# One kernel of three transformer blocks: the expert stage split further and loaded by halves, and a small store issued by another engine

## Time and profile before

| | |
|---|---|
| median of 3 runs | 3319.97 us (3319.68 to 3324.28) |
| profiled execution | 3321.52 us, span 3319.7 us |
| mean granted TensorE clock | 0.965 |
| TensorE busy | 3104.9 us, 94% |
| VectorE, ScalarE, GpSimd busy | 1830.9, 1596.4, 737.2 us |
| DMA | 693.72 MB, mean 209 GB/s |

### The profile page before, as it was taken

One profiled execution on the slowest core, in us unless ns is written; L12 is line 12 of the kernel. 1 busy time (PEld: TensorE's weight loads), 2 busy tenths in 40 slices (PEclk: granted clock), 3 DMA queues, 4 the chain that ended last, 5 costly groups with the idle time before them and its releaser, 6 DMA issues. The chain is left out here.

```text
span 3319.7 us, 39152 instructions
## 1 busy us (share of the span) xinstructions
PE 3104.9 (94%) x14036; PEld 2408.6 (73%) x14036; DVE 1830.9 (55%) x2216; ACT 1596.4 (48%) x2141; POOL 737.2 (22%) x379
## 2 busy tenths in 40 slices
PE   7986999998999999989997888999999999999997
PEld 6754678877877787768885666777777777777753
DVE  3257433344367404440031447887888888888773
ACT  4334434433566423232231325766766766666652
POOL 2400144442523344324442330000000000000020
PEclk9987999999999999999998898999999999999998
DMA  3243322222222132212224317999999999999971
GB/s 148 102 161 119 127 76 101 101 89 89 77 76 76 52 114 77 102 51 101 89 108 191 153 51 318 402 408 411 406 407 412 405 408 411 406 407 411 411 262 45
DMA packets 65594, 693.72 MB, mean 209 GB/s; under 512 B 6912, under 2 KB 7296, under 8 KB 25440
## 3 DMA queue, kind: packets, MB, share of 16 engines
q1 hardware_dynamic: 54336, 650.05, 49.8%
q0 software_dynamic: 6912, 25.17, 2.0%
q10 hardware_dynamic: 4256, 17.30, 1.3%
HBM read 654.22 MB, written 38.27 MB: 209 GB/s over the span
## 5 line engine op out<-in xcount | busy, mean ns | idle before, releaser
L142 POOL TENSOR_TENSOR ring_low<-ring,mix_ring_high 128x1024 fp32r<-128x1024 f32 x120 | 292.4, 2470 | 455.2 <-ACT mix_ring_high L137 455.2
L213 PE MATMUL psum<-mix_high,mix_ring_high 128*128 128x512 f32 x864 | 342.9, 397 | 13.1 <-DVE h_low L507 8.6
L215 PE MATMUL psum<-mix_high,ring_low 128*128 128x512 f32 x864 | 337.1, 390 | 0.0
L213 PE MATMUL psum<-ex_high,ex_rows_high 128*128 128x512 f32 x768 | 314.9, 410 | 1.5 <-DVE ex_rows_low L2823 1.4
L215 PE MATMUL psum<-ex_high,ex_rows_low 128*128 128x512 f32 x768 | 299.7, 390 | 0.0
L214 PE MATMUL psum<-h_low,mix_ring_high 128*128 128x512 f32 x736 | 287.2, 390 | 0.0
L142 POOL TENSOR_TENSOR ring_low<-ring,ff_ring_high 128x1024 fp32r<-128x1024 f32 x72 | 175.0, 2464 | 415.0 <-ACT ff_ring_high L137 224.7
L2510 POOL CAST ex_index<-table 128x1 uint32 (+1 forms) x32 | 5.9, 184 | 1090.2 <-PE psum L2550 1032.5
L2854 DVE TENSOR_TENSOR ring_low<-ring,ex_high 128x2048 fp32r<-128x2048 f32 x96 | 214.4, 2287 | 38.7 <-ACT ex_high L2686 38.6
L2854 DVE TENSOR_TENSOR ex_more_low<-ex_more,ex_high_in_x 128x2048 fp32r<-128x2048 f32 x96 | 219.5, 2287 | 19.9 <-ACT ex_high_in_x L2686 19.9
L2605 PE MATMUL psum<-ex_more,ex_act_t 128*128 128x512 f32 x512 | 224.9, 592 | 0.0
(11 more groups left out here) (581 smaller groups left out, 6884.8 us busy)
## 6 DMA issues: line engine op xcount, KB each, us to landing
ex_more<-moe_w SPq DMA_DIRECT2D x128, 2048.0 KB, 9.3
ring<-wstream SPq DMA_DIRECT2D x87, 2048.0 KB, 8.4
ring<-moe_w SPq DMA_DIRECT2D x64, 2048.0 KB, 10.5
ex_bias_up<-moe_b SPq DMA_DIRECT2D x32, 1024.0 KB, 9.6
y_rows<-mx_zero ACTq DMA_DIRECT2D x1, 16384.0 KB, 44.5
y_rows<-ex_y SPq DMA_DIRECT2D x32, 512.0 KB, 10.5
x<-xt SPq DMA_DIRECT2D x8, 256.0 KB, 6.1
rel<-rel_bias SPq DMA_DIRECT2D x1, 2048.0 KB, 9.7
```

Source lines behind the costliest of these rows:

```text
L142: e.tensor_tensor(low, full, high.bitcast(F32), ALU.subtract).then_inc(self.low_ready, 1)
L213: pe.matmul(out, a[0], b[0], start=start, stop=False)
L215: return pe.matmul(out, a[1], b[0], start=False, stop=stop)
```

## The change

- All 24 quarters are split. `PIECES` gets the last halves of s = 4 and 5 as four more quarters, after the first halves of both, the plain products and `act_t` go, and `act_high`, `act_low` are made for both halves. `RING` is 12; two new slots lie in h, so ScalarE waits in the opening block for the store of the tokens (`x_stored`).
- The gate's bias comes by a product: `picks_bias` (64 x 128, ones in the rows of the expert and zeros elsewhere) times `gate_bias` (the 32 experts' biases, high parts in rows 0 to 31, low parts in 32 to 63) opens the PSUM sums of s = 0 and 2. GpSimd rewrites `picks_bias` for each block from `owner`. ScalarE's Silu reads PSUM directly; the gate's limit is applied behind it, as a limit of its Silu, in the last instruction of `take_up`; 1/1.702 moves to `take_y`. `take_gate` goes. The DMA that spreads biases carries `up` alone.
- Each piece is loaded as two transfers of 1 MB, each after its own two quarters are used.
- In the mixer stage the second DMA of zeros is issued by SP, after its panel loads.

The core of the diff:

```diff
+SILU_LIMIT = SW_ALPHA * SW_LIMIT / (1.0 + float(np.exp(-SW_ALPHA * SW_LIMIT)))
...
                 ring.load_until(sp, min(n0 + 4 + SLOTS, FIRST["ple_proj"]))
+                sp.wait_ge(zeroed, 1)
+                sp.dma_start(r.y_dram[0:ROWS, :], zero[:, :]).then_inc(r.blanked, 16)
                 sp.wait_ge(r.blanked, 32)
...
                 first, count = S * TOPE // ROWS + 1, TABLE - S * TOPE // ROWS
                 act.dma_start(r.y_dram[first * ROWS:(first + count) * ROWS, :].rearrange("(b p) d -> p b d", p=ROWS),
                                zero[:, :].rearrange("p (a d) -> p a d", a=1).to_broadcast([P, count, D])).then_inc(r.blanked, 16)
-                act.dma_start(r.y_dram[0:ROWS, :], zero[:, :]).then_inc(r.blanked, 16)
                 norm.preload(act)
                 norm.root(act)
...
-    RING = 10
-    PIECES = tuple((s, c) for s in range(4) for c in range(PARTS)) + tuple((s, c) for s in (4, 5) for c in range(2))
+    RING = 12
+    PIECES = tuple((s, c) for s in range(4) for c in range(PARTS)) + tuple((s, c) for half in (0, 2) for s in (4, 5) for c in (half, half + 1))
     NQ, NP = len(PIECES), len(PIECES) // 2
     place = {q: n for n, q in enumerate(PIECES)}
-    act_at, dve_at = (8, 14), (10, 14, 18)
+    act_at, dve_at = (8, 16), (16, 22)
+    HALVES = tuple((s, c // 2) for s, c in PIECES if c % 2 == 0)
+    half_of = lambda i: slice(i * KT * PANEL // 2, (i + 1) * KT * PANEL // 2)
...
+        gate_bias = nc.alloc_sbuf_tensor_at("ex_gate_bias", [2 * NE, D], F32R, offset=r.bias_at + 4 * D)
+        high_in_x = nc.alloc_sbuf_tensor_at("ex_high_in_x", [P, 4, PART], F32R, offset=g.x_at)
+        high_in_h = nc.alloc_sbuf_tensor_at("ex_high_in_h", [P, 2, PART], F32R, offset=g.h_at)
...
-                for s in range(6):
-                    sp.dma_start(piece(s), g.extra["moe_w"][s, :, :]).then_inc(landed[s], 16)
+                for i in range(2):
+                    sp.dma_start(bias_raw[i * NE:(i + 1) * NE, :], g.extra["moe_b"][:, 0:D]).then_inc(bias_in, 16)
+                for s, i in HALVES:
+                    sp.dma_start(piece(s)[:, half_of(i)], g.extra["moe_w"][s, :, half_of(i)]).then_inc(landed[s][i], 16)
 
                 def spread_up(e):
-                    sp.dma_start(bias_up[:, :], g.extra["moe_b"][e, 0:2 * D].partition_broadcast(P)
+                    sp.dma_start(bias_up, g.extra["moe_b"][e, D:2 * D].partition_broadcast(P)
                                  .rearrange("p a f -> p (a f)")).then_inc(up_in, 16)
...
-                    for s in range(6):
-
-                        if s < 4:
-                            sp.wait_ge(used, b * NQ + place[s, PARTS - 1] + 1)
-                        else:
-                            sp.wait_ge(dn_done, b * 2 + s - 3)
-                        sp.dma_start(piece(s), g.extra["moe_w"][bass.ds(e * 6 + s, 1), :, :].rearrange("a p f -> (a p) f"))\
-                            .then_inc(landed[s], 16)
-                        if s == 3:
+                    for s, i in HALVES:
+                        sp.wait_ge(used, b * NQ + place[s, 2 * i + 1] + 1)
+                        sp.dma_start(piece(s)[:, half_of(i)],
+                                     g.extra["moe_w"][bass.ds(e * 6 + s, 1), :, half_of(i)].rearrange("a p f -> (a p) f"))\
+                            .then_inc(landed[s][i], 16)
+                        if (s, i) == (3, 1):
                             sp.wait_ge(h_done, b * 2 + 2)
                             spread_up(bass.ds(e, 1))
...
+                def pick_bias(after, at):
+                    pool.wait_ge(used, after * NQ + NQ + place[2, 0] + 1)
+                    pool.tensor_copy(picks_bias[:, :], owner[:, at].to_broadcast([2 * NE, P])).then_inc(picks_set, 1)
+                    pool.wait_ge(picks_set, after + 2)
+
+                pool.wait_ge(owner_set, 1)
+                pick_bias(0, slice(1, 2))
                 with pool.Fori(1, blocks_of(pool)) as b:
                     pool.wait_ge(rows_in, b * 16)
                     pool.wait_ge(x_turned, b * 2 + 2)
                     gather(b + 1, bass.ds(b + 1, 1))
+                    pick_bias(b, bass.ds(b + 1, 1))
...
-                                            low_piece(s)[:, k * PANEL:(k + 1) * PANEL]), k == 0, k == KT - 1)
+                                            low_piece(s)[:, k * PANEL:(k + 1) * PANEL]), k == 0 and s not in (0, 2), k == KT - 1)
...
+                    pe.wait_ge(picks_set, b + 1)
                     for s in range(4):
-                        pe.wait_ge(taken, b * 4 + s + 1)
+                        pe.wait_ge(up_taken if s % 2 else gate_taken, b * 2 + s // 2 + 1)
+                        if s % 2 == 0:
+                            pe.matmul(psum[:, s, :], picks_bias[:, :], gate_bias[:, 256 * s:256 * s + 512], start=True, stop=False)
...
-                    pe.wait_ge(a_ready, b + 1)
+                    pe.wait_ge(a_low, b * 2 + 2)
                     for s in (4, 5):
-                        for k in range(4, KT):
-                            mm = pe.matmul(psum[:, s + 2, :], act_t[:, k - 4, :], weights(s, k), start=False, stop=k == KT - 1)
-                        mm.then_inc(dn_done, 1)
+                        for c in range(2, PARTS):
+                            quarter(b, s, c, psum[:, s + 2, :], act_high, act_low)
...
+                def high_act(b, c):
+                    act.wait_ge(h_turned, b * 2 + c + 1)
+                    act.activation(act_high[:, 4 * c:4 * c + 4, :].rearrange("p k s -> p (k s)"), psum[:, 4, :], ACT.Copy).then_inc(a_high, 1)
 
                 def take_y(b):
                     act.wait_ge(y_out, b * 16 + 16)
                     for s in range(2):
-                        act.wait_ge(dn_done, b * 2 + s + 1)
-                        act.activation(y[:, 512 * s:512 * s + 512], psum[:, 6 + s, :], ACT.Copy).then_inc(y_done, 1)
+                        act.wait_ge(used, b * NQ + place[4 + s, PARTS - 1] + 1)
+                        act.activation(y[:, 512 * s:512 * s + 512], psum[:, 6 + s, :], ACT.Copy, scale=1.0 / SW_ALPHA).then_inc(y_done, 1)
 
                 def sigmoid(b, c):
-                    act.wait_ge(limited, b * 2 + c + 1)
+                    act.wait_ge(used, b * NQ + NQ + place[2 * c, PARTS - 1] + 1)
                     act.wait_ge(h_done, b * 2 + c + 2)
-                    act.activation(sig[:, :], gate[:, :], ACT.Silu, scale=SW_ALPHA).then_inc(sig_ready, 1)
+                    act.activation(sig[:, :], psum[:, 2 * c, :], ACT.Silu, scale=SW_ALPHA).then_inc(gate_taken, 1)
...
+                        if opening and n == 10:
+                            act.wait_ge(x_stored, 16)
                         if n == act_at[1]:
                             sigmoid(b, 0)
-                        if c == 0:
-                            act.wait_ge(landed[s], b * 16 + 16)
+                        if c % 2 == 0:
+                            act.wait_ge(landed[s][c // 2], b * 16 + 16)
...
+                    high_act(b, 0)
                     sigmoid(b, 1)
                     act.wait_ge(x_turned, b * 2 + 3)
                     high_rows(0, 5)
-                    take_act(b)
+                    high_act(b, 1)
                     act.wait_ge(x_turned, b * 2 + 4)
                     high_rows(1, 5)
...
+                act.wait_ge(bias_in, 32)
+                act.activation(gate_bias[:, :], bias_raw[:, :], ACT.Copy).then_inc(bias_high, 1)
                 norm.root(act)
...
+                    for i, ends in enumerate((first, upto)):
+                        link(dve.tensor_tensor(owned[:, :], ends[:, :], stacked[:, :], ALU.mult))
+                        link(dve.tensor_reduce(owner_first[:, i:i + 1], owned[:, :], AX_X, ALU.add))
+                    iota = g.block_iota[0:2 * NE, :]
+                    link(dve.tensor_scalar(owner[:, :], iota, owner_first[0:2 * NE, 1:2], None, ALU.is_lt))
+                    dve.scalar_tensor_tensor(owner[:, :], iota, owner_first[0:2 * NE, 0:1], owner[:, :], ALU.is_ge, ALU.mult).then_inc(owner_set, 1)
...
-                def take_gate(b, c):
-                    dve.wait_ge(used, b * NQ + NQ + place[2 * c, PARTS - 1] + 1)
-                    dve.wait_ge(up_in, b * 16 + 16)
-                    dve.tensor_tensor(gate[:, :], psum[:, 2 * c, :], bias_up[:, 512 * c:512 * c + 512], ALU.add).then_inc(taken, 1)
-                    dve.wait_ge(taken, b * 4 + 2 * c + 5)
-                    dve.tensor_scalar(gate[:, :], gate[:, :], SW_LIMIT, None, ALU.min).then_inc(limited, 1)
 
                 def take_up(b, c):
                     dve.wait_ge(used, b * NQ + NQ + place[2 * c + 1, PARTS - 1] + 1)
-                    dve.scalar_tensor_tensor(up[:, :], psum[:, 2 * c + 1, :], 1.0, bias_up[:, D + 512 * c:D + 512 * c + 512], ALU.add, ALU.add)\
-                        .then_inc(taken, 1)
-                    dve.wait_ge(taken, b * 4 + 2 * c + 6)
+                    dve.wait_ge(up_in, b * 16 + 16)
```

(43 more changed lines are left out.)

62 lines of the change are left out of this document (31 added, 31 removed).

## The result

The changed kernel takes **3290.95 us** (median of 4 runs, 3289.41 to 3292.39), against 3319.97: a ratio of 0.991, 95% interval 0.9892 to 0.9927. It is 29.0 us faster, where 58.4 were forecast, and 3290.95 lies above the range of 3252 to 3279.

A forecast was written before the change was run, and what follows sets the result against it. TensorE was taken to set each of 32 expert blocks, and a held ScalarE to cost some 31 us in the mixer stage; -31.4 - 30.7 + 3.7 = -58.4 us gave 3262, range 3252 to 3279.

The forecast's parts named there:

- Part 3: Expert stage, TensorE: the two gate-bias products of 512 columns cost 0.45 us a block together (bounds 0 and 1.7).
- Part 1: Mixer stage: the small store of zeros leaves ScalarE, so its square root starts earlier: -31.4 us (-25 to -33).
- Rival A: Mixer stage: the large DMA holds ScalarE whatever comes behind it, so moving the store gives 0: 3293 us, chance 0.11.
- Part 2: Expert stage, TensorE: the last four quarters split, 24 products in place of 16 passes: -1.41 us a block.
- Part 4: Expert stage, VectorE: 32.4 of 35.0 us busy, tight order holding by 0.2 us; taken as 0, 9 us if it fails.
- Part 5: Expert stage: ScalarE busy some 29 of 35 us, GpSimd copies the bias picks in idle time; cost 0.
- Part 6: Expert stage, DMA: loads by halves and half of the spread bias cost 0, bound +7 us.
- Rival C: Expert stage: half-size transfers lose rate, 370 GB/s, a block takes 38.3 us: 3364 us, chance 0.05.
- Rival B: Expert stage: VectorE or the DMA engines bound the block: 3269 to 3278 us, chance 0.18.
- Part 7: Opening of the expert stage: bias loads before ScalarE's root, VectorE's instructions before the marks and its longer queue: +3.7 us (0.5 to 6).

## Why the prediction was wrong, step by step

**Part 3 failed, by the size of one term.** "I take 0.45 us for both, since the types are those of the split ones (bounds 0 and 1.7)": the two products cost 1.20 us a block. With it the prediction's own sum is 35.96 - 1.41 + 1.20 = 35.75, and 35.77 was measured. The missed 0.75 makes 32 x 0.75 = 24 of the 29 us between forecast and result. The mechanism, that TensorE sets the block, was right; the type was the wrong thing to look at for the price. What is priced apart is that 64 rows stand between products of 128 (shown: 128 and 96 rows cost 0.22 to 0.24, a second product of 64 rows 0.28, two together one change-over). The Trainium skill, "TensorEngine Tiling (Array Packing)", section "Tiling Modes" (Key Properties), says that going to another tiling mode, and not only to another tile, drains TensorE, and its list of forms has one of 64 rows and none of 96. The runs agree in which heights pay, 64 and not 96, and show 0.40 us for a way in and out; of a drain itself they show only the weight loads that don't start ahead. The bound of 1.7 held this case, but the range did not reach to it: with 1.7 for both, 32 x 1.25 = 40 us more, its upper end would have been past 3300. The bound was written down and then left out.

**Part 1, -31.4, measured -30.7 in the stage itself.** The root comes 2.55 us behind the first store's issue, and 2.54 were worked out; that it stands at 1804.43 and not at 1803.75 is the 0.7 of the untouched stages. The missing 0.7 is behind the root. Everything up to the first product was said to hang on the root alone, but eight products that spread the averages were done long before it while ScalarE was held. Now they run just ahead of the eight that spread the reciprocals, x16 in one row where the earlier trace rows has x8: the last of them ends 3.35 us behind the root instead of 2.64. The zeros did delay a panel, by 2.5 us, and as forecast that cost nothing; the small store needs 10.5 us to land, not the 2 named for it, and had the cover. Rival A (a large DMA holds whatever follows) is refuted: the table load starts 0.04 us behind the 0.44 of L2323. That A's 3293 is near the result is chance: it had the wrong half missing. The rule of the Trainium skill, "DMA: Bandwidth & Descriptors", section "SWDGE vs HWDGE vs iDMA", that issuing from several engines saves little, would have missed the whole gain of this edit; measured by itself it is 30 us, and that decides.

**Part 2, -1.41, measured -1.39** (34.57 - 35.96). **Part 4** held: the second transposes of the activations came 6.43 us behind the first, against 6.42 worked out, so VectorE's tail with its 0.2 us was in time, in a block of 35.0 too; 32.5 us busy there, 32.4 worked out. **Part 5** held in the block, ScalarE 27.4, below the 29 said; but GpSimd's copy of the picks, costed at nothing, brings the 2.2 us of the last stage's start. **Part 6** held: halves landed in 7.4 us and ScalarE didn't wait. Rival C is refuted: 407 and 408 GB/s with halves at 35.0 us, and 409 to 411 in the kernel without bias products. Rival B would soon have been right: by our estimate 14.16 MB at 410 GB/s need 34.5 us a block, and VectorE's tail is felt at 34.57.

**Part 7, +3.7, measured +4.6**, and made up otherwise. The root's part was +1.4 (ScalarE is idle for 4.79 us until the biases land, then copies them for 1.06), +1.0 in the forecast. The marks were to add 1.3 and added 0.4: TensorE's sum of the table starts 50.09 us into the stage before and 51.85 after. The sum took 5.58 us instead of 3.99, with a granted clock of 0.65 over it instead of 0.93: +1.6, not in the forecast. What follows adds 1.3, with 1.4 forecast. So that it is off by 0.9 only is luck.

**The last stage was given nothing in the sum, and lost 3.4**: 2.2 to GpSimd, and 1.2 behind its first root. There the granted clock of the 30 us behind the root is 0.89, where the kernel before had 0.94 (the changed kernel, then the one before):

```profile
3182.89:3212.89 30.00, 24.66 (x76) 13.60 (x75) 18.29 (x33) 19.73 (x42) 5.28 (x5) 0.89 0.54 198
```

```profile
3213.22:3243.22 30.00, 26.30 (x83) 13.23 (x82) 18.28 (x33) 19.71 (x42) 5.29 (x5) 0.94 0.55 195
```

Four traces have the 0.89 (the changed kernel, that without bias products, that with 96 rows, that with whole pieces), and take 107.7 to 108.1 us from this root to the end; the eight with 0.94 take 106.0 to 106.8. So the 1.2 goes with the clock; why it fell once more in these four, no run shows.

## What to carry to other kernels

Before a small product goes between large ones, look at its height: with 64 contracted rows beside 128, pad it with rows of zeros or gather such products in one place, and price a change of form, not columns. Put a small DMA ahead of a large one on a queue, or on another. A bound that one writes down for an unknown price, times the number of blocks, must be inside the range.

## What the runs showed that was not expected

- A product of 512 columns that contracts 64 rows costs 0.60 to 0.63 us between products of 128 rows; padded with zeros to 96 or 128 rows, 0.22 to 0.24.
- Going from 128 rows to 64 and back keeps two weight loads from starting ahead, and shows as busy time of the products: TensorE read 36.00 of 36.00 with 0.8 us of it lost in each block. Only the rows of the weight loads have an idle time.
- A copy added to GpSimd's loop, idle time before and after it, made the engine's first instruction of the next stage 2.2 to 2.6 us later.
- In the opening, steps made 1.5 to 2 us shorter brought nothing, as a later step of small products fell into a stretch at the lower clock: 5.96 us at a granted 0.60 instead of 4.19 at 0.88.
- The kernels' first 1800 us, with no edit in them, differ by up to 4.1 us between executions: effects of 1 or 2 us are read from one instruction of a trace to another, not from the start or the total.
